# Token dispatch to expert-sorted rows in place of seven one-hot gathers

## The reference

```python
def moe_swiglu(h, w_router, w_gu, w_down):
    logits = (ht @ w_router).astype(jnp.float32)
    top_val, top_idx = lax.top_k(logits, TOP_K)
    top_w = jax.nn.softmax(top_val, axis=-1)
    gates = jnp.sum(jax.nn.one_hot(top_idx, N_EXPERTS) * top_w[..., None], axis=1)
    for e in range(N_EXPERTS):
        out = out + gates[:, e:e + 1] * swiglu(ht, w_gu[e], w_down[e])
```

## Time and profile before

| | |
|---|---|
| median of three runs | 1671.63 us (1667.96, 1671.63, 1672.0) |
| time of the profiled execution | 1677.78 us |
| its span, first to last instruction | 1675.7 us |
| mean granted TensorE clock, share of full | 0.991 |
| busy: PE, DVE, ACT, POOL | 1632.1, 1292.1, 1048.1, 90.6 us |
| read from memory, written | 452.69 MB, 1.05 MB |

### The profile page before, as it was taken

How to read it: one execution, slowest core, us unless ns; L and a number is a source line. 1 busy time by engine, 2 the same in 40 slices (tenths; PEclk the granted TensorE clock), 3 DMA queues, 4 the chain that set the end, 5 groups by cost and what they waited for, 6 DMA issues and landing times.

```text
span 1675.7 us, 22727 instructions
## 1 busy us (share of the span) xinstructions
PE 1632.1 (97%) x8581; PEld 1375.1 (82%) x8581; DVE 1292.1 (77%) x1126; ACT 1048.1 (63%) x927; POOL 90.6 (5%) x105
## 2 busy tenths in 40 slices
PE   6999999999999998999999999999999999999997
PEld 5888789999788886888888888888888888888886
DVE  4865685555585577988888888888888888888886
ACT  4454653333544564777777777777777777776774
POOL 5402000100220001000000000000000000000000
PEclk9999999999999999999999999999999999999998
DMA  9545355555553347999999999999998998998980
GB/s 282 195 131 107 120 173 179 187 191 178 159 192 101 96 175 295 339 371 344 344 372 336 351 371 329 356 372 324 362 371 320 366 372 319 368 371 321 367 320 27
DMA packets 222177, 454.65 MB, mean 271 GB/s; under 512 B 8576, under 2 KB 62368, under 8 KB 222112
## 3 DMA queue, kind: packets, MB, share of 16 engines
q1 hardware_dynamic: 220800, 450.95, 75.9%
q0 software_dynamic: 1024, 2.10, 1.0%
q10 hardware_dynamic: 288, 0.72, 0.1%
HBM read 452.69 MB, written 1.05 MB: 271 GB/s over the span
## 4 chain that ended last, share of the span: by engine, by line
PE 93%; DVE 3%; DMA 1%; ACT 1%; issue 1%; POOL 1%; SPq 0%; ACTq 0%; POOLq 0%; DVEq 0%
PE bank L1242 28%; PE bank L1243 28%; PE bank L1244 28%; PE bank L1278 2%; PE bank L1264 2%; PE bank L1478 2%; PE bank L1516 1%; DMA w_slot<-in_w_in 1%; PE bank L1559 1%; PE bank L1293 1%; DVE w_slot_lo L387 1%; ACT w_hi L380 0%; PE bank L1357 0%; DVE probT_area L905 0%; DVE gate_area L928 0%
## 5 line engine op out<-in xcount | busy, mean ns | idle before, releaser
L387 DVE TENSOR_TENSOR w_slot_lo<-w_slot,w_hi 128x2048 fp32r<-128x2048 f32 (+1 forms) x429 | 972.2, 2275 | 217.6 <-ACT w_hi L380 216.0
L380 ACT CAST w_hi<-w_slot 128x2048 fp32r<-128x2048 f32 x429 | 816.2, 1905 | 324.9 <-PE bank L1244 311.6
L1242 PE MATMUL bank<-w_hi,a_hi 128*128 128x512 f32 x1208 | 480.0, 397 | 11.1 <-DVE w_slot_lo L387 5.0
L1243 PE MATMUL bank<-w_slot_lo,a_hi 128*128 128x512 f32 x1208 | 477.2, 395 | 0.0
L1244 PE MATMUL bank<-w_hi,a_lo 128*128 128x512 f32 x1208 | 475.4, 394 | 0.0
L1242 PEld LDWEIGHTS bank<-w_hi,a_hi 128*128 128x128 f32 x1208 | 228.6, 189 | 62.6 <-DVE w_slot_lo L387 12.6
L1244 PEld LDWEIGHTS bank<-w_hi,a_lo 128*128 128x128 f32 x1208 | 227.9, 189 | 50.2
L1243 PEld LDWEIGHTS bank<-w_slot_lo,a_hi 128*128 128x128 f32 x1208 | 228.2, 189 | 47.0
L1243 PE MATMUL bank<-w_slot_lo,b_hi 128*128 128x512 f32 x448 | 176.3, 394 | 0.0
L1242 PE MATMUL bank<-w_hi,b_hi 128*128 128x512 f32 x448 | 176.1, 393 | 0.0
L1244 PE MATMUL bank<-w_hi,b_lo 128*128 128x512 f32 x448 | 175.2, 391 | 0.0
(11 more groups left out here) (158 smaller groups left out, 1374.6 us busy)
## 6 DMA issues: line engine op xcount, KB each, us to landing
w_slot<-in_moe_w_gu SPq DMA_DIRECT2D x224, 1024.0 KB, 5.2
w_slot<-in_moe_w_down SPq DMA_DIRECT2D x112, 1024.0 KB, 5.0
w_slot<-in_w_in SPq DMA_DIRECT2D x44, 1024.0 KB, 5.1
w_slot<-in_ffn_w_gu SPq DMA_DIRECT2D x22, 1024.0 KB, 5.1
w_slot<-in_ffn_w_down SPq DMA_DIRECT2D x11, 1024.0 KB, 4.9
w_slot<-in_w_out SPq DMA_DIRECT2D x8, 1024.0 KB, 5.0
w_slot<-in_w_branch SPq DMA_DIRECT2D x8, 768.0 KB, 4.5
bias_sb<-in_na_rpb POOLq DMA_DIRECT2D x32, 64.0 KB, 6.5
```

Source lines behind the costliest of these rows:

```text
L380: nc.scalar.copy(hi_slot[n % HI_RING][:, 0:WIDTH[n]], raw[:, 0:WIDTH[n]]).then_inc(hi_ready, 1)
L387: eng.tensor_tensor(lo, raw, hi, ALU.subtract).then_inc(lo_ready, 1)
L1242: nc.tensor.matmul(place, lhs[0], rhs[0], start=first, stop=False)
L1243: nc.tensor.matmul(place, lhs[0], rhs[1], start=False, stop=False)
```

## The change

A table `picked_rows` of 1024 + 512 rows of 1024 floats is made in device memory: row 128 e + r is for the token of rank r in expert e. In the dense feed-forward of layer 0, ACT issues four transfers that fill its first 1024 rows with zeros. After the router GpSimd works out each token's two row numbers with small operations, and sends each token's row of `h` to both with four indirect transfers of 128 rows. A rank of 128 or more goes to one of 512 spare rows. In each of the first seven experts, after weight tile 21, SP loads the next expert's 128 rows (512 KB) into `picked`, an unused half of the storage of `a_hi`. PE transposes them, 8 transposes, in place of the gather. Expert 0 and the second round still use `gather`. DVE keeps `is_first` and `is_second` unweighted for GpSimd and signals `ranks_ready`.

The diff, cut to its core:

```diff
+C_SPARE = C_IOTA8 + EXPERTS
+C_BAND = C_SPARE + 2 * BLOCKS
+C_ZERO = C_ROPE + 2 * 2 * BLOCKS * HEAD
+C_END = C_ZERO + D_MODEL
+NO_ROW = EXPERTS * SLOTS
...
-        a_hi, a_lo = sb("a_hi", DC * SEQ, F32R), sb("a_lo", DC * SEQ, F32R)
+        (a_raw, a_hi), a_lo = sb_split("a", DC * SEQ), sb("a_lo_part", DC * SEQ, F32R)
+        picked_rows = nc.dram_tensor("picked_rows", (NO_ROW + 2 * SEQ, D_MODEL), F32).ap()
+        picked = a_raw[:, DC * SLOTS:DC * SLOTS + D_MODEL]
...
+            def load_picked(item, e):
+                by_expert = picked_rows[0:NO_ROW, :].rearrange("(e t) n -> e t n", t=SLOTS)
+                sp.wait_ge(dispatched, 16 * 2 * BLOCKS)
+                sp.wait_ge(picked_done, item * 2 + 2)
+                sp.dma_start(picked, by_expert[e + 1]).then_inc(picked_loaded, 16)
+
-            def load_rest(item, e):
+            def load_rest(item, e, pick_next=False):
                 for j in range(MOE_RING, MOE_TILES):
                     sp.wait_ge(w_used, moe_used(item, j - MOE_RING))
                     load_tile(j, e)
+                    if pick_next and j == MOE_TILES // 2:
+                        load_picked(item, e)
...
+            own(nc.gpsimd.tensor_scalar(row_at, iota8.unsqueeze(1).broadcast_to([P, BLOCKS, EXPERTS]),
+                                        float(SLOTS), None, ALU.mult))
+            pool.wait_ge(ranks_ready, 1)
+            ranks = rank_x.rearrange("p e b -> p b e")
+            own(nc.gpsimd.tensor_tensor(row_at, row_at, ranks, ALU.add))
+            own(nc.gpsimd.tensor_scalar(rank, ranks, float(SLOTS), 2.0 * NO_ROW, ALU.is_ge, ALU.mult))
+            own(nc.gpsimd.tensor_tensor(row_at, row_at, rank, ALU.add))
+            for k, onehot in enumerate((is_first, is_second)):
+                own(nc.gpsimd.tensor_tensor(row_of[:, k], row_at, onehot, ALU.mult))
+            for n in (EXPERTS // 2, EXPERTS // 4, 1):
+                v = row_of.rearrange("p k b e -> p (k b) e")
+                total = row_f.unsqueeze(2) if n == 1 else v[:, :, 0:n]
+                own(nc.gpsimd.tensor_tensor(total, v[:, :, 0:n], v[:, :, n:2 * n], ALU.add))
+            for i in range(2 * BLOCKS):
+                own(nc.gpsimd.tensor_scalar(rows_i[:, i:i + 1], row_f[:, i:i + 1], spare_row[:, i:i + 1], None, ALU.min))
+            pool.wait_ge(rows_zeroed, 16 * 4)
+            pool.wait_ge(h_scaled, BLOCKS)
+            for k in range(2):
+                for b in range(BLOCKS):
+                    i = k * BLOCKS + b
+                    nc.gpsimd.indirect_dma_start(picked_rows, bass.IndirectOffsetOnAxis(ap=rows_i[:, i:i + 1], axis=0),
+                                                 h[:, b, :], None).then_inc(dispatched, 16)
...
+                        if layer == 0 and 2 <= s < 6:
+                            n = EXPERTS // 4
+                            act.dma_start(
+                                picked_rows[(s - 2) * n * P:(s - 1) * n * P, :].rearrange("(e p) n -> p e n", p=P),
+                                constants[:, C_ZERO:C_END].unsqueeze(1).broadcast_to([P, n, D_MODEL]))\
+                                .then_inc(rows_zeroed, 16)
...
-            own(nc.vector.tensor_scalar(rank_x, rank.rearrange("p b e -> p e b"), -1000.0, None, ALU.add))
+            nc.vector.tensor_scalar(rank_x, rank.rearrange("p b e -> p e b"), -1000.0, None, ALU.add).then_inc(ranks_ready, 1)
+            dve.wait_ge(ranks_ready, 1)
...
-            def first_picks(item):
+            def picked_transposes(item):
+                pe.wait_ge(picked_loaded, item * 16)
+                for c in range(DC):
+                    last = nc.tensor.transpose(bank[4 + c // 4][:, (c % 4) * SLOTS:(c % 4 + 1) * SLOTS],
+                                               picked[:, c * P:(c + 1) * P], ident)
+                    if c % 4 == 3:
+                        last.then_inc(picked_done, 1)
+
+            def first_picks(item, first):
                 pe.wait_ge(h_scaled, BLOCKS)
                 gather(item)
...
                 if more:
-                    gather(item + 1)
+                    picked_transposes(item + 1) if first else gather(item + 1)
```

More of the change, by code:

```diff
@@ L72 @@
 C_IOTA8 = C_IOTA + SLOTS
-C_BAND = C_IOTA8 + EXPERTS
+C_SPARE = C_IOTA8 + EXPERTS
+C_BAND = C_SPARE + 2 * BLOCKS
 C_MOD4 = C_BAND + BLOCKS * SEQ
@@ L163, in build @@
     assert ND % HI_RING == 0 and MOE_TILES % HI_RING == 0 and MOE_TILES % MOE_RING == 0 and MOE_TILES % 2 == 0
-    attn_slots = (C_END - C_BAND + BLOCKS * KV_W + QK_HEADS // 2 * SEQ + BLOCKS * NA_HEADS * SEQ + 6 * SEQ
+    attn_slots = (C_ZERO - C_BAND + BLOCKS * KV_W + QK_HEADS // 2 * SEQ + BLOCKS * NA_HEADS * SEQ + 6 * SEQ
                   + 8 * BLOCKS * HEAD) // TILE
@@ L214, in build @@
         most = sb("most", 1, I32)
+        rows_f = sb("rows_f", 3 * BLOCKS * EXPERTS + 2 * BLOCKS)
+        rows_i = sb("rows_i", 2 * BLOCKS, I32)
+        picked_rows = nc.dram_tensor("picked_rows", (NO_ROW + 2 * SEQ, D_MODEL), F32).ap()
         with ExitStack() as early:
-            attn_cst = sb("attn_cst", C_END - C_BAND, F32, early)
+            attn_cst = sb("attn_cst", C_ZERO - C_BAND, F32, early)
             v_area = sb("v_area", BLOCKS * KV_W, F32, early)
@@ L276, in build @@
         iota = cst[:, C_IOTA:C_IOTA + SLOTS]
+        spare_row = cst[:, C_SPARE:C_BAND]
         iota8 = cst[:, C_IOTA8:C_IOTA8 + EXPERTS]
@@ L281, in build @@
         colmask = attn_cst[:, C_COLM - C_BAND:C_ROPE - C_BAND]
-        rope_cs = attn_cst[:, C_ROPE - C_BAND:].rearrange("p (r s b d) -> p r s b d", r=2, s=2, b=BLOCKS)
+        rope_cs = attn_cst[:, C_ROPE - C_BAND:C_ZERO - C_BAND].rearrange("p (r s b d) -> p r s b d", r=2, s=2, b=BLOCKS)
         ffn_act = [score_area[:, i * 512:(i + 1) * 512] for i in range(2)]
@@ L303, in build @@
         rank_x, gate_x = [v.rearrange("p b e -> p (b e)").rearrange("p (e b) -> p e b", b=BLOCKS) for v in (rank_t, gate_t)]
+        two = 2 * BLOCKS
+        row_of = rows_f[:, 0:two * EXPERTS].rearrange("p (k b e) -> p k b e", k=2, b=BLOCKS)
+        row_at = rows_f[:, two * EXPERTS:(two + BLOCKS) * EXPERTS].rearrange("p (b e) -> p b e", b=BLOCKS)
+        row_f = rows_f[:, (two + BLOCKS) * EXPERTS:]
         def pick_tile(i):
@@ L341, in build @@
         gain_row_loaded, h_scaled = sem("gain_row_loaded"), sem("h_scaled")
+        rows_zeroed, ranks_ready, dispatched, picked_loaded = (
+            sem("rows_zeroed"), sem("ranks_ready"), sem("dispatched"), sem("picked_loaded"))
         banks_read = sem("banks_read")
@@ L430, in passes, with one_round @@
         def passes(eng, first_picks, body, next_round=None):
-            def one_round(first_item):
-                first_picks(first_item)
+            def one_round(first_item, first):
+                first_picks(first_item, first)
                 with eng.Fori(0, EXPERTS - 1) as e:
-                    body(first_item + e, e, True)
-                body(first_item + (EXPERTS - 1), EXPERTS - 1, False)
-            one_round(0)
+                    body(first_item + e, e, True, first)
+                body(first_item + (EXPERTS - 1), EXPERTS - 1, False, first)
+            one_round(0, True)
             if OVER:
@@ L447, in passes @@
                             next_round(r)
-                        one_round(r * EXPERTS)
+                        one_round(r * EXPERTS, False)
         @block.sync
@@ L480, in _ @@
                         .then_inc(qk_gain_loaded, 16)
-                    sp.dma_start(attn_cst[:, :], constants[:, C_BAND:]).then_inc(cst_loaded, 16)
+                    sp.dma_start(attn_cst[:, :], constants[:, C_BAND:C_ZERO]).then_inc(cst_loaded, 16)
                     sp.dma_start(cst[:, C_TRI:], constants[:, C_TRI:C_BAND]).then_inc(cst_loaded, 16)
@@ L513, in load_rest, with load_round @@
                     load_tile(j, e)
-            def load_round(first_item):
+                    if pick_next and j == MOE_TILES // 2:
+                        load_picked(item, e)
+            def load_round(first_item, first):
                 with sp.Fori(0, EXPERTS - 1) as e:
-                    load_rest(first_item + e, e)
+                    load_rest(first_item + e, e, first)
                     load_first(first_item + e, e + 1)
@@ L530, in _ @@
                 load_tile(j, 0)
-            load_round(0)
+            load_round(0, True)
             if OVER:
@@ L537, in _ @@
                         load_first(r * EXPERTS - 1, 0)
-                        load_round(r * EXPERTS)
+                        load_round(r * EXPERTS, False)
             sp.wait_ge(x_final, 1)
@@ L817, in picked_hi_part, with expert @@
                                    bank[4 + g][:, :]).then_inc(picked_hi, 1)
-            def first_picks(item):
+            def first_picks(item, first):
                 split.moe(item, 3)
                 picked_hi_part(item)
-            def expert(item, e, more):
+            def expert(item, e, more, first):
                 def act_hi_part(f):
@@ L1117, in _ @@
```

(9 more changed lines are left out.)

1 line of the change is left out of this document (removed).

## The result

| | before | after |
|---|---|---|
| median of the runs | 1672.0 us (5) | 1665.05 us (5) |
| ratio after to before, 95% interval | | 0.9945 [0.9929, 0.9961] |
| profiled execution, its span | 1677.78, 1675.7 | 1667.44, 1665.5 |
| mean granted clock | 0.991 | 0.991 |
| read from memory, written | 452.69 MB, 1.05 MB | 460.55 MB, 7.34 MB |

The kernel is 7 to 9 us faster, beyond its uncertainty.

The account below looks back on a forecast made before the run. PE was taken to bound the kernel, holding 93% of the chain of waits. Boundaries -1.4, clock falls +3.3 and dispatch +0.3 summed to +2.2 us on the median of 1671.63: 1673.8, range 1668 to 1680.5.

Parts of the forecast that it names:

- What is late next: Expert boundaries: scatter waits for y_lo, gate tile for bank 2's add; 0.2 us saved each, -1.4 over seven.
- The 0.08 that I took back for the restart: Gate tile at each boundary: after a wait the next matmul starts 0.31 us later, not 0.23.
- the chain that I had named: Boundary: ACT's y_hi, weight tile and a_hi, then DVE's a_lo and add of bank 2, ending at 5.06 us.
- Rival C: Boundaries: PE's saving counts; near 1665.7 us by the scatter alone, 1652.8 if y were early too; chance 0.08.
- The clock: PE idle at seven boundaries: two or three falls to a lower clock at 1.3 us each, +3.3 us.
- Rival B: Boundaries, between transposes and scatter: the clock falls at each of seven, +8.0 us, 1679.6; chance 0.20.
- The fall behind the second: Clock fall near 431 us, at the second norm: nine matmuls took 3.96 us in place of 2.07, so 1.9.
- Zeros: Dense feed-forward: four 1 MB transfers issued by ACT cost nothing; at most 21 us if the cover were gone.
- Dispatch: Start of expert 0: GpSimd's small operations and DVE delay each other, +0.3 us, between 0 and 2.
- Rival D: Expert 0: dispatch or its traffic holds it up, PE waits 10 to 20 us, about 1687; chance 0.06.
- rival A: Boundaries: PE stalls but the clock holds, -1.4 + 0.3, 1670.5 us; chance 0.18.
- within 0.3%: Whole kernel: time not distinguishable from no change, 1666.6 to 1676.6 us; chance 0.67.

Follow-up runs that it names:

- The swaps: ACT rounds the picked tokens ahead of the third weight tile: changed kernel, 1658.44 us; kernel before with slots 6 to 13 moved, 1663.57 us.
- ACT's swap: Changed kernel with ACT rounding the picked tokens ahead of the third weight tile at each boundary: 1658.44 us, ratio 0.9901.

## Why the prediction was wrong

**Where it was right.** What is late next: scatter at 2.4, gate tile at 5.11 (measured 2.43 and 5.12), eight transposes at 0.11, and that PE's saving of 2.69 shrinks to some tenths. The term was -1.4 us, with a bound of -2.4; at equal placement, against the gather put back, it measured -1.3. The 0.08 that I took back for the restart is there too (0.34 in place of 0.23 behind the gate tile's first matmul), inside the expert's time. The swaps confirm the chain that I had named, and its counterpart in the kernel before. Rival C, that PE's saving counts, did not happen. That the time came out near its 1665.7 is chance.

**The step that failed** is one that the sum does not have. I priced each added instruction and transfer, and took the products, whose experts fill 96% of the stage, as unchanged. "No cost" for new buffers was not even written down. That term measured -10.9 us and is larger than all the others. The diff showed it could be there: two new buffers and wider constants ahead of the slots. The trace of before showed its size: 227 and 232 ns a matmul in neighbouring tiles, at the same clock and both fully busy. I read durations of the costly groups only as means over all slots.

**The clock.** The forecast counted two or three falls, +3.3 us. This term was wrong too: at the boundaries there were none in the changed kernel, nor with the slots moved back. I had weighed the gaps by pattern, two of four stretches; but the last scatter, which I put on the same footing, has no transposes ahead of it, and taking six of eight away brought four falls in seven. So the mechanism exists, the eight transposes keep clear of it, and a fall costs 0.7 to 1.1 here and not 1.3 (1.3 at the first norm). Rival B falls with it. One trace was also too little to weigh the norms by: in the thirteen traces of this document the clock fell behind the first norm in 4, behind the second in 11 and behind the third in 2. The fall behind the second, which I priced at 1.9 from the products alone, costs 2.4: without it, with the gather back, the stage to the third norm took 217.9 us in place of 220.3.

**The rest.** Zeros: 0 forecast, none measured. Dispatch: +0.3 forecast; expert 0 took 118.00 as the others did, and from the third norm to its first product it took 19.0 us, as before. The +1.8 ahead of expert 0 arose earlier, 1.3 of it by the fall at the first norm. Two of GpSimd's small operations did sit out DVE's tiles as feared, at no cost to the path, and issuing the four indirect transfers took 1 to 3 us each:

```profile
665.60 2.21 POOL L675 TENSOR_SCALAR route<-route 128x16 f32<-128x16 f32 x1
...
673.58 3.10 POOL L690 DMA_INDIRECT picked_rows<-h_sb,rows_i  x1 [0.53 <-POOL rows_i L684]
...
680.27 2.08 POOL L690 DMA_INDIRECT picked_rows<-h_sb,rows_i  x1 [0.30 <-issue]
```

The last ends at 682.4, 17.5 us after the ranks were ready (664.9), and SP issued the load of the picks at 694.4: no stop of SP is seen. Rival D falls.

**Had placement been left alone**, the runs say 0.9994 [0.9982, 1.0007] for the change, about 1671. That is rival A, to which I had given 0.18: the stall without the falls, 1670.5. (The run's own median of 1673.63 stands beside 1674.68 for the kernel before; that it meets the forecast's 1673.8 is chance.) The verdict "within 0.3%" would have been right for the change's work, and was wrong for the kernel as built.

## What to carry to other kernels

Before pricing what a change does, list what it moves: every buffer allocated ahead of a hot one shifts it, and here 32 bytes were worth 11 us, some eight times the 1.3 of the intended effect. Compare a kernel with its change at equal placement (pads of 32 bytes do it), and look for steps that differ between slots of one ring; a busy share of 100% hides them. And when two chains of different engines are nearly equal, shorten both: transposes and ACT's swap gave some 0.3 and 0.00 us a boundary alone, 0.83 together.

## What the runs showed of the hardware

- The start of an SBUF buffer modulo 64 bytes changes the pace of float32r products of 512 columns in which it is the streamed operand: 227 ns a matmul at 0, 232 at 32 (weight slots, moved both ways above); how is open. The Trainium skill, "SBUF — State Buffer", section "Operand start alignment", asks only for a multiple of the element size and says that it is about legality and timed nothing; both places are legal here, and the times differ.
- With the rounded weights at 32, which no transfer touches, an expert took 2.9 us more. Products of 256 columns, in which they are the operand loaded beforehand, went from 120 to 117 ns.
- The clock held through seven stretches with 1.8 us of idle in 5.1 us (1.40 and 0.37 in the rows above) where eight transposes stood in them, and fell in four of seven without six of these. A fall cost 0.7 to 1.1 us at a boundary, 1.3 at the first norm and 2.4 at the second.
- A GpSimd operation of 16 elements a partition, beside a weight tile on DVE, took 2.21 us where its neighbours took 0.2 to 0.5.
